# A hybrid hyena, retention and latent-attention backbone on one core: the order of the opening, and the first loads of the hyena stage

## The reference

```
h = sin(f0 * (z @ w1 + b1));  h = sin(f1 * (h @ w2 + b2));  h = (h @ w3) * exp(-t * deltas)
kern = both sides of h;       kern = kern / sum(|kern|)
spectrum = rfft(kern)                                   # one per layer, and one for the context
z = x1 * long_conv(short_conv(v), spectrum[0]);  y = x2 * long_conv(z, spectrum[1])
```

## Time and profile before

| | us |
|---|---|
| median of 3 runs | 4182.84 |
| lowest and highest | 4176.96, 4186.05 |
| the profiled execution's own time | 4174.05 |
| its span, first to last instruction | 4172.0 |
| opening, to the last fold | 0 to 235.7 |
| hyena stage of layer 0 | from 1132.8 |
| hyena stage of layer 1 | from 3159.7 |

### The profile page before, as it was taken

One profiled execution on the slowest core, in us unless ns is written; L12 is line 12 of the kernel. 1 busy time (PEld: TensorE's weight loads), 2 busy tenths in 40 slices (PEclk: granted clock), 3 DMA queues, 4 the chain that ended last, 5 costly groups with the idle time before them and its releaser, 6 DMA issues. The chain is left out here.

```text
span 4172.0 us, 53362 instructions
## 1 busy us (share of the span) xinstructions
PE 3658.4 (88%) x19724; PEld 3077.3 (74%) x19724; DVE 2192.2 (53%) x3864; ACT 1430.2 (34%) x2818; POOL 1141.2 (27%) x1017
## 2 busy tenths in 40 slices
PE   6879976888767889999999899769896879999998
PEld 2568975777656778888888779758785667888886
DVE  4468435666575154444444573357675634454454
ACT  1241124666522142222222421247672222222222
POOL 1112110111200235544445421101110024455454
PEclk9989977999978989999999999779998999999999
DMA  5145200000144021111111152000004321111111
GB/s 187 73 163 187 88 4 28 1 14 1 63 157 153 25 69 40 31 35 35 40 40 40 66 188 78 3 26 6 6 6 182 108 79 53 48 49 51 40 50 55
DMA packets 154422, 267.88 MB, mean 64 GB/s; under 512 B 9112, under 2 KB 121129, under 8 KB 151818
## 3 DMA queue, kind: packets, MB, share of 16 engines
q1 hardware_dynamic: 149020, 223.65, 16.3%
q0 software_dynamic: 5232, 41.95, 2.5%
HBM read 230.15 MB, written 35.42 MB: 64 GB/s over the span
## 5 line engine op out<-in xcount | busy, mean ns | idle before, releaser
L2627 POOL TENSOR_TENSOR x<-x,mlp_tmp 128x512 f32<-128x512 f32 x576 | 785.4, 1396 | 807.4 <-DVE mlp_tmp L2608 802.2
L2608 DVE TENSOR_TENSOR mlp_tmp<-psum,gate 128x512 f32<-128x512 f32 x576 | 391.5, 688 | 273.3 <-POOL x L2627 194.7
L152 PE MATMUL psum<-act_hi,w_hi 128*128 128x512 f32 (+1 forms) x1280 | 473.2, 370 | 12.5 <-DVE w_lo L2586 12.5
L153 PE MATMUL psum<-act_lo,w_hi 128*128 128x512 f32 (+1 forms) x1280 | 473.0, 369 | 0.0
L154 PE MATMUL psum<-act_hi,w_lo 128*128 128x512 f32 (+1 forms) x1280 | 472.7, 369 | 0.0
L152 PE MATMUL psum<-w_hi,hidden_hi 128*128 128x512 f32 x1152 | 450.0, 391 | 0.0
L153 PE MATMUL psum<-w_lo,hidden_hi 128*128 128x512 f32 x1152 | 448.6, 389 | 0.0
L154 PE MATMUL psum<-w_hi,hidden_lo 128*128 128x512 f32 x1152 | 448.3, 389 | 0.0
L2600 DVE TENSOR_TENSOR hidden_lo<-square,hidden_hi 128x512 fp32r<-128x512 f32 x160 | 102.3, 639 | 594.1 <-ACT hidden_hi L2572 594.1
L2564 ACT ACTIVATE relu<-psum 128x512 f32<-128x512 f32 x160 | 88.8, 555 | 667.8 <-PE psum L154 667.8
L1722 DVE TENSOR_REDUCE att_max<-psum 128x1 f32<-128x512 f32 (+2 forms) x272 | 217.8, 801 | 178.8 <-PE psum L154 178.6
(11 more groups left out here) (342 smaller groups left out, 7970.0 us busy)
## 6 DMA issues: line engine op xcount, KB each, us to landing
w_raw<-in_mlp_w SPq DMA_DIRECT2D x128, 512.0 KB, 3.8
side_w<-in_w_ada SPq DMA_DIRECT2D x40, 1024.0 KB, 6.4
w_raw<-in_w_in SPq DMA_DIRECT2D x32, 512.0 KB, 4.9
hy_ahead<-in_hy_ahead POOLq DMA_DIRECT2D x8, 2048.0 KB, 20.7
open_tab<-in_hy_ahead POOLq DMA_DIRECT2D x8, 1024.0 KB, 15.4
ada_w<-in_w_ada SPq DMA_DIRECT2D x8, 1024.0 KB, 12.9
spec_scratch<-open_staged SPq DMA_DIRECT2D x16, 512.0 KB, 2.7
x<-in_x SPq DMA_DIRECT2D x4, 2048.0 KB, 12.8
```

Source lines behind the costliest of these rows:

```text
L152: pe.matmul(out, lhs[0], rhs[0], start=start, stop=False)
L153: pe.matmul(out, lhs[0], rhs[1], start=False, stop=False)
L2608: dve.tensor_tensor(tmp[:, j % 2, :], ps[:, 4 + j % 4, :], gate[:, int(t >= LAT_TILES), 512 * h:512 * h + 512], ALU.mult).then_inc(gated.s ...
L2627: pool.tensor_tensor(a, a, tmp[:, j % 2, :], ALU.add).then_inc(added.sem, 1)
```

## The change

1. In the opening POOL waits for the last small load (`f_in["w3"]`) before it issues the tables.
2. PE makes all three `second` before the first `chunk`. Two chunks, not four, stand before the first taps; one goes with each of the five taps, the last behind them. DVE's `add_bias` calls move likewise, and it reduces the second layer's arguments without a chunk between them.
3. In the fold loop `taps` of the next unit come ahead of `fold` of this one (on ACT `high` ahead of `even_part`, on DVE `low` ahead of `both_parts`). The normalisers are made in the filter tile's own banks, after the first fold of the unit, and only the taps that reuse these banks wait for `norm_read`.
4. The loads of `x` are issued by ACT after the last fold of the third unit, no longer by SP, and SP doesn't wait for them at the end.
5. In `phase_latent` POOL issues, once the last head group's tiles are all made, the V stream (now at 16 KB, in the place of the second table piece) and the first piece of `ahead[0]`.
6. In `phase_hyena` SP issues the first spectrum first, then X1, the context, X2, the second spectrum. POOL issues the context's tables at once, the other three pieces of `ahead[0]` and `behind[0]` only when V is convolved.

```diff
 phase_open, SP
-                if f == ((1, 1), 0):
-                    sp.wait_ge(folded.sem, folded[((1, 0), K - 1)])
...
-            for s in x_in:
-                sp.wait_ge(s.sem, s[0])
 phase_open, PE
             def taps(g):
-                if i and norm_after(gens[i - 1]):
-                    pe.wait_ge(norm_read.sem, norm_read[norm_after(gens[i - 1])[-1]])
+                if i >= 2 and norm_after(gens[i - 2]):
+                    pe.wait_ge(norm_read.sem, norm_read[norm_after(gens[i - 2])[-1]])
             def norm(l, s, g):
-                bank = 2 * ((G[g] + 1) % 2)
+                bank = norm_bank(g)
-            chunk(0)
             for c in range(3):
                 second(c)
-                chunk(c + 1)
+            chunk(0)
+            chunk(1)
             for j, g in enumerate(tiles_of[units[0]]):
                 taps(g)
-                if 4 + j < n_chunks:
-                    chunk(4 + j)
+                chunk(2 + j)
+            chunk(n_chunks - 1)
             turn(n_chunks - 1)
             for n, u in enumerate(units):
+                done = tiles_of[units[n]][-1]
                 for j, f in enumerate(tiles_of[u]):
+                    if j < len(after):
+                        taps(after[j])
+                    if j == 0:
+                        pe.wait_ge(pm_lo.sem, pm_lo[done])
...
                     fold(f)
-                    if j < len(after):
-                        taps(after[j])
+                    if j == 0:
+                        for l, s in norm_after(done):
+                            norm(l, s, done)
 phase_open, ACT
+            act.wait_ge(folded.sem, folded[((1, 0), K - 1)])
...
 phase_open, POOL
+            pool.wait_ge(f_in.sem, f_in["w3"])
             for kt in range(K):
                 pool.dma_start(tab[0][:, kt, 0:4], io["hy_ahead0"][:, kt, 0:4]).then_inc(tab_in[kt].sem, 16)
 phase_latent, POOL, after the last copy of the rotated keys
+                if g == HEAD_GROUPS - 1:
+                    pool.wait_ge(made.sem, made[(g, ALL_TILES - 1)])
+                    hyena_first_loads(kit, l, pool)
+def hyena_first_loads(kit, l, pool):
+    ahead, v_in = kit.at("hy_ahead0", [P, 4, 8, 512], 0, F32R), kit.at("hy_in", [P, 2, SEQ + 2], 16)
+    v_rows = kit.hy_dram[2 * HY_W:3 * HY_W, 0:SEQ].rearrange("(c p) n -> p c n", p=P)
+    pool.dma_start(v_in[:, :, 1:SEQ + 1], v_rows).then_inc(kit.sig("hy_v_got", 16, fresh=True).sem, 16)
+    pool.dma_start(ahead[:, 0], kit.io["hy_ahead0"][:, 0]).then_inc(kit.sig("hy_tab0_in", 16, fresh=True).sem, 16)
 phase_hyena, SP
-            rows((0, V))
+            spectrum(steps[0])
             rows((0, X1))
...
             rows((0, X2))
-            spectrum(steps[0])
             spectrum(steps[1])
 phase_hyena, POOL
-            pool.dma_start(ahead[0][:, 0], io["hy_ahead0"][:, 0]).then_inc(tab_in[0].sem, 16)
...
+            pool.wait_ge(conved.sem, conved[((0, V), 1)])
             for kt in (1, 2, 3):
                 pool.dma_start(ahead[0][:, kt], io["hy_ahead0"][:, kt]).then_inc(tab_in[kt].sem, 16)
```

More of the change, by code:

```diff
@@ L289, in _ @@
             for f in odd_folds:
-                if f == ((1, 1), 0):
-                    sp.wait_ge(folded.sem, folded[((1, 0), K - 1)])
-                    for i in range(2):
-                        sp.dma_start(x[:, 4 * i:4 * i + 4, :],
-                                     io["x"][0, 512 * i:512 * i + 512].rearrange("(t p) n -> p t n", p=P)).then_inc(x_in[i].sem, 16)
-                    sp.dma_start(x[:, 8:10, :], io["ctx"][0].rearrange("(t p) n -> p t n", p=P)).then_inc(x_in[2].sem, 16)
                 (l, _), kt = f
@@ L350, in norm @@
             def norm(l, s, g):
[L352 removed]
+                bank = norm_bank(g)
                 pe.wait_ge(ksummed.sem, ksummed[g])
[L354 to L355 removed]
+                pe.wait_ge(pm_lo.sem, pm_lo[g])
+                pe.wait_ge(absed.sem, absed[g])
                 for i in range(4):
@@ L407, in _ @@
                         pe.wait_ge(odd_tab_in.sem, odd_tab_in[K - 1])
+                    fold(f)
                     if j == 0:
-                        pe.wait_ge(pm_lo.sem, pm_lo[tiles_of[u][-1]])
-                    fold(f)
-                    if j < len(after):
-                        taps(after[j])
+                        for l, s in norm_after(done):
+                            norm(l, s, done)
                 for g in after[len(tiles_of[u]):]:
                     taps(g)
-                if after:
-                    for l, s in norm_after(after[-1]):
-                        norm(l, s, after[-1])
         @block.scalar
@@ L449, in _ @@
                 for j, f in enumerate(tiles_of[u]):
+                    if j < len(after):
+                        high(after[j])
                     if u[1] == 0:
                         even_part(f)
-                    if j < len(after):
-                        high(after[j])
                 for g in after[len(tiles_of[u]):]:
                     high(g)
+            act.wait_ge(folded.sem, folded[((1, 0), K - 1)])
+            for i in range(2):
+                act.dma_start(x[:, 4 * i:4 * i + 4, :],
+                              io["x"][0, 512 * i:512 * i + 512].rearrange("(t p) n -> p t n", p=P)).then_inc(x_in[i].sem, 16)
+            act.dma_start(x[:, 8:10, :], io["ctx"][0].rearrange("(t p) n -> p t n", p=P)).then_inc(x_in[2].sem, 16)
             act.wait_ge(norm_read.sem, norm_read[(1, 0)])
@@ L567, in _ @@
             dve.tensor_tensor(w3[:, 1, :], fwd, bwd, ALU.subtract).then_inc(w3_ready.sem, 1)
-            for c in range(3):
-                reduce_argument(0, c)
+            for n in range(2):
+                for c in range(3):
+                    if n:
+                        dve.wait_ge(sined.sem, sined[(0, c)])
+                    reduce_argument(n, c)
             dve.wait_ge(small_in.sem, small_in[2])
             add_bias(0)
-            for c in range(3):
-                dve.wait_ge(sined.sem, sined[(0, c)])
-                reduce_argument(1, c)
-                add_bias(c + 1)
+            add_bias(1)
             dve.wait_ge(d_in.sem, d_in[1])
@@ L592, in _ @@
                         decays(after[j])
+                        low(after[j])
                     if u[1] == 1:
                         both_parts(f)
-                    if j < len(after):
-                        low(after[j])
+                    if j == 0:
+                        for l, s in norm_after(done):
+                            invert(l, s, done)
                 for g in after[len(tiles_of[u]):]:
@@ L599, in _ @@
                     low(g)
-                if after:
-                    for l, s in norm_after(after[-1]):
-                        invert(l, s, after[-1])
 TWO_PI = 2 * math.pi
@@ L1935, in phase_hyena @@
     invs = [(ct, par) for par in range(2) for ct in range(2)]
-    got = {key: kit.sig(f"hy_got{i}", 16) for i, key in enumerate(u_in)}
+    got = {key: kit.sig(f"hy_got{i}" if i else "hy_v_got", 16) for i, key in enumerate(u_in)}
     for sg in got.values():
```

15 lines of the change are left out of this document (8 added, 7 removed).

## The result

The changed kernel takes 4114.66 us in the median of 4 runs (4110.27 to 4118.64), the kernel before 4179.9 us beside it on the same chip (4172.01 to 4186.05, 4 runs). The ratio is 0.9845, 95% interval 0.9823 to 0.9867: 65 us faster, where 64.9 were forecast (4118, range 4104 to 4139). The profiled execution took 4111.42, its span is 4109.6, so the pair of traces differs by 62.4 us.

What follows compares the result with a forecast made beforehand. The prediction held that queue order, not the engines, limits the opening and hyena stages. Gains of 30.9 (opening), 17.3 and 16.7 (hyena layers 0 and 1) sum to 64.9, from 4182.84 to 4118 us; range 4104 to 4139.

Steps and rivals of the forecast that it cites:

- Up to the first taps: Opening: small loads go alone with tables held back, two chunks bind; first taps at 46.3, 8.1 us earlier.
- Taps with chunks: Opening, first taps to first fold: five rounds and the last chunk take 33.6 us for 32.8, 0.8 lost.
- The folds: Opening's fold stage: taps ahead of folds remove holes and slow-clock folds; 124.9 us for 148.5, 23.6 less.
- Loads of x at zero: End of opening: x loads issued by ACT lie beside unit 4; zero cost, 3 us if that cover is gone.
- Hyena, layer 0: Layer 0 hyena stage: first products 18.7 us earlier, less half of 2.8 for the second spectrum; 17.3 gained, bounds 9 and 20.
- Hyena, layer 1: Layer 1 hyena stage: forward starts 9.0 us earlier, DVE multiplies at 3185.6, not 3202.3; 16.7 gained, bounds 9 and 17.
- rival A: Hyena stages: tables, asked for later, become the bound and delay steps; total gain 49 us, 4134; chance 0.14.
- Latent stage: Latent stage: two more POOL issues and 3.1 MB of loads, where DMA is next to unused, cost zero.
- B: Hyena stages: DVE holds up POOL's table issue, at most 13 us and 7.6; total gain 54, 4129; chance 0.07.
- C: Opening: tables starve chunk 0, first taps no earlier than now; total gain 57 us, 4126; chance 0.07.
- D: Fold stage: thin taps and one-column matmuls keep PE's clock low; 25 us slower, 4208; chance 0.03.
- E: Opening gains, hyena stage doesn't, early loads coming at the stage's end; total gain 44 us, 4139; chance 0.03.

Runs made afterwards that it cites:

- e2: Changed kernel without POOL's wait for the last small load, so the tables are issued at once; 4115.08 us, ratio 0.9849.
- e9: Kernel of e7 with the normalisers inside the fold, between its halves, and DVE's inverse ahead of combining the parts; 4112.69 us, ratio 0.9841.
- e12: Kernel of e11 with a second staging buffer for the spectrum in the last unit; 4096.45 us, ratio 0.9804.
- e11: Changed kernel with the edits of e8, e9 and e10 together; 4099.28 us, ratio 0.9805.
- e4: Changed kernel with the second spectrum issued by SP right behind X1, ahead of the context's rows and X2; 4118.18 us, ratio 0.9864.
- e5: Changed kernel with V and first table piece loaded in the hyena stage again, other tables not held back, spectrum still first; 4151.91 us, ratio 0.9941.
- e6: Changed kernel with the first spectrum behind X2 again in SP's queue, V and first table still early; 4128.15 us, ratio 0.9884.
- e1: Changed kernel with the whole opening of the kernel before, the hyena parts kept; 4144.57 us, ratio 0.9921.
- e8: Changed kernel with tables held until the fourth chunk landed, three chunks made between second-layer steps, decays and odd tables issued later; 4106.55 us, ratio 0.9834.
- e7: Changed kernel, but a unit's first fold waits only for its last latent tile's low part, the context's fold for the context tile's; 4115.69 us.
- e10: Changed kernel with the three loads of x issued one fold apart, not at once; 4115.50 us, ratio 0.9847.

## Why the prediction came out right

**The forecast case happened, and each of its three regions is within 2 us**: opening 29 to 30 for 30.9, hyena stages 17.4 and 17 for 17.3 and 16.7. Inside the opening and inside the hyena stage of layer 0 it was right partly by errors that cancel, which is luck.

*Up to the first taps.* Forecast 46.3, found 43.6. The small loads came at 6.2, as said. The step that failed is "chunk 0 lands at about 36.5, chunk 1 landed meanwhile": chunk 0 was there at 31.7 (the prediction's own terms, 8, 26.7 and 1.2, give 35.9, not 36.5): from 8 to 14 us SP's queue moved 520 packets and POOL's 127 (275 and 277 before), and chunk 1 was the late one, a wait of 2.79 us. The every-second-packet rule of the earlier trace rows held afterwards: 846 and 844 packets from 14 to 30. The prediction put the 8 us down to both, the held tables and the chunk order; e2 shows it is the order, nearly alone. The forecast's 46.3 lies within the 43.2 to 46.7 of the eight traces, so the 2.7 us are no more than executions differ by.

*Taps with chunks.* 33.2 us from the first taps to the next unit's for 33.6: right, with rounds of 5.67.

*The folds.* Unit 1 took 33.9 (76.85 to 110.73), as said. The hole of 1.1 for the last tile's low part is there to a tenth. Unit 2 is what failed: the clock. From the next unit's first taps (76.85) to the last fold's end (205.9) it took 129.0 us where the prediction had 124.9, and unit 2 alone 40.7 for 36.9. The prediction held the bound "if the normalisers' matmuls of one column let the clock fall, two folds cost 1.6 more each": the fold behind the hole of 1.1, a taps and another fold did, 1.5 + 1.8 + 1.4, and the wait for DVE was 1.25 and not 0.4, while the 16 matmuls themselves took 1.8 and not 3.4, being at full clock. The other 1.1, in front of 200.15, is the next paragraph's; against it stands the last normaliser, 0.9 for 1.9. What lets the clock fall stays open: behind the 16 matmuls with no hole it fell in e9 and e12 and not in e11, and behind the hole of 1.12 in three of seven traces. The prediction also put the last hole of before at 6.2 us, where the trace has 6.6; its sum doesn't use it.

*Loads of x at zero.* They are hidden for ACT, but not for the stores: DVE waits 6.3, 1.2, 2.4 and 1.9 us for its staging buffer while they run, PE 1.1, and from the last matmul to the next stage it is 6.6 us for 5.7. That is 2 us where the prediction had nothing; its 3 us "if that cover is gone" was for ACT's squares, another mechanism. e12 shows the cause, one staging buffer, and removes it.

*Hyena, layer 0.* X1 released ACT 7.9 us in (8 said), forward 16.8 in (16.6), products 25.35 (25.5). For the second spectrum the prediction took half of 2.8 us, its upper bound; the wait is 4.45, beyond it. The spectrum landed 40.4 us into the stage, with the last of the tables at 40.2 (40.0 by that bound), and DVE was ready for it at 36.0 and not at 37.2. Up to the second step's multiply the stage had gained 15.4 us; that the sum is 17.4 all the same comes from 2 us gained behind it, for which the prediction has no term and the runs no cause. e4 shows that a place further ahead in SP's queue doesn't cure the wait. e5 and e6 bear out the mechanism in the main: without the early 3.1 MB and the tables held back the gain is gone, and in layer 0 the spectrum's place carries 10 of it. Which of the first two does how much isn't shown.

*Hyena, layer 1.* X1 6.6 in (6.7), forward 15.6 in (15.6), products 23.9 in (24.5), no wait: right. "`behind[0]`: hidden" was not quite: PE waits for it 1.7 us here and 2.4 in layer 0. That and the 4.45 us of layer 0 are what came of rival A; the 49 it gave are excluded by the result.

*Latent stage.* V and the first table piece had landed by 925.6, 181 us ahead of the stage that needs them: zero, as said.

*The rivals.* B, POOL's issue held by DVE: the six table issues took 0.55 us in the median and at most 0.60 (in the kernel before 0.55 to 0.60), in layer 1 with DVE convolving from 3123.07, beside the last of the three and `behind[0]`, and the second piece landed 9.0 us after its issue, no later than the 11.7 of the earlier trace rows. The Trainium skill's rule on DVE blocking POOL's descriptors ("SBUF — State Buffer", the box on how DVE blocks DMA) made no difference that shows; whether the convolutions run in such a mode, no run here shows. C, chunk 0 starved: it came earlier, and chunk 1 at 39.9, not 48. D: the clock was low for 10 us in the fold stage and cost 4.7, not 90. E: excluded by e1.

## What to carry to other kernels

When work is moved ahead of a stage, ask what the queue is short of: here it was bytes in front of the first product (e5, e6), and the order among the rest was worth nothing (e4). A wait that holds back a big transfer can be worth nothing where what it protects isn't what is late (e2), and the same wait, held longer and with work ready to use what then lands early, 8 us (e8). A hole removed on PE is worth its length only if what follows isn't set by another engine (e7): take the chain of waits as one, and look at the clock behind each. What one trace shows of the clock behind a short hole is not yet a rule: look for the same hole in the traces of other runs.

## What the runs showed of the hardware

- Two DMA queues with work moved the same number of packets, 846 and 844 in 16 us, with packets of 1 KB and 8 KB, so that SP's queue moved 0.85 MB and POOL's 5.64. Alone the queue of small packets moved 5.79 MB in 16 us (e8), 362 GB/s against some 410 for both.
- TensorE's clock fell to 1.2 GHz behind holes of 1.12 (at 113.84), 1.25 (with the normalisers ahead of it), 1.89, 2.42 and 2.83 us, and behind 16 matmuls of one column with no hole at all (e9, 117.24 on). It did not fall behind the hole of 1.11 at 200.15, nor behind that of 1.5 in e10, nor behind the 8 matmuls of one column of layer 1. The same code didn't always do the same: behind the hole of 1.12 the clock fell in three traces (changed, e4, e6) and not in four (e2, e5, e8, e10), behind the 16 matmuls with no hole in e9 and e12 and not in e11. It stayed low for 3 to 10 us each time. What tells these cases apart is open.
- The time of one program differs from run to run by up to 16 us (4111 to 4127 in e4, 4091 to 4101 in e11). From the end of the opening to the first hyena stage e1 took 7.2 us longer than the kernel before with nearly the same code, by stretches at the lower clock; an effect under 4 us was read from traces, not from medians.
